# A new layout in device memory for the expert gate values

## What is computed

```python
q = (tok @ wq).reshape(-1, PEER_HEADS, 2, PEER_SUB_DIM)
s1 = jnp.einsum("nhd,kd->nhk", q[:, :, 0], k1)      # 128 keys each side
s2 = jnp.einsum("nhd,kd->nhk", q[:, :, 1], k2)
v1, i1 = lax.top_k(s1, 16);  v2, i2 = lax.top_k(s2, 16)
cand = (v1[..., :, None] + v2[..., None, :]).reshape(-1, 8, 256)
top_s, top_c = lax.top_k(cand, 16)
expert = i1[top_c // 16] * 128 + i2[top_c % 16]
gate = jax.nn.softmax(top_s, axis=-1)
act = jax.nn.gelu(x . u[expert])
out = sum_e (gate * act) * v[expert]
```

## Time and profile before

| | |
|---|---|
| executions timed | 3748.21, 3754.81, 3764.75 us |
| profiled execution, first to last instruction (span) | 3746.2 us |
| TensorE matmul busy | 3568.6 us (95%) |
| TensorE weight load busy | 3086.4 us (82%) |
| VectorE busy | 2356.7 us (63%) |
| ScalarE busy | 1525.1 us (41%) |
| GpSimd busy | 1025.7 us (27%) |
| data moved by DMA | 566.25 MB in 245131 packets |

### The profile page before, as it was taken

How to read it: one execution, slowest core, us unless ns; L and a number is a source line. 1 busy time by engine, 2 the same in 40 slices (tenths; PEclk the granted TensorE clock), 3 DMA queues, 4 the chain that set the end, 5 groups by cost and what they waited for, 6 DMA issues and landing times. The chain is left out here.

```text
span 3746.2 us, 46716 instructions
## 1 busy us (share of the span) xinstructions
PE 3568.6 (95%) x18068; PEld 3086.4 (82%) x18068; DVE 2356.7 (63%) x3934; ACT 1525.1 (41%) x2054; POOL 1025.7 (27%) x678
## 2 busy tenths in 40 slices
PE   7999999979999999999999999999999998699998
PEld 6888777768888889999999999987778887678886
DVE  6655544445469998777657777666565576856354
ACT  5555554445342224444533333335443224434232
POOL 1222222127137775555411111110020014311002
PEclk9999999989999999999999999999999999999999
DMA  5111111036336675677599999861123332132331
GB/s 187 51 51 51 37 51 51 23 133 215 107 103 229 236 242 183 257 261 266 205 332 310 306 312 310 299 214 49 55 91 102 96 96 54 37 98 85 101 96 62
DMA packets 245131, 566.25 MB, mean 151 GB/s; under 512 B 91648, under 2 KB 133904, under 8 KB 242736
## 3 DMA queue, kind: packets, MB, share of 16 engines
q1 hardware_dynamic: 203968, 396.31, 32.9%
q0 software_dynamic: 37440, 135.32, 10.2%
q10 hardware_dynamic: 3504, 31.65, 2.1%
HBM read 497.36 MB, written 60.82 MB: 149 GB/s over the span
## 5 line engine op out<-in xcount | busy, mean ns | idle before, releaser
L1398 PE MATMUL peer_banks<-peer_h_parts,peer_w_parts 128*128 128x448 f32 (+1 forms) x3456 | 735.7, 372 | 11.4 <-POOL peer_w_parts L1679 5.6
L1398 PEld LDWEIGHTS peer_banks<-peer_h_parts,peer_w_parts 128*128 128x128 f32 x3456 | 647.3, 189 | 79.9 <-POOL peer_w_parts L1679 14.2
L1398 PE MATMUL peer_banks<-peer_act_parts,peer_w_parts 128*128 128x448 f32 x3072 | 624.7, 365 | 1.0 <-DVE peer_act_parts L2118 0.8
L1398 PEld LDWEIGHTS peer_banks<-peer_act_parts,peer_w_parts 128*128 128x128 f32 x3072 | 576.4, 188 | 47.1 <-DVE peer_w_parts L2123 1.7
L1851 ACT ACTIVATE peer_w_parts<-slots 128x1024 fp32r<-128x1024 f32 x272 | 287.1, 1056 | 430.0 <-PE peer_banks L1398 415.6
L1398 PE MATMUL ffn_ps<-h_parts,ffn_w_parts 128*128 128x512 f32 x1920 | 441.4, 392 | 18.2 <-DVE h_parts L2736 10.9
L1679 POOL TENSOR_TENSOR peer_w_parts<-slots,peer_w_parts 128x1024 fp32r<-128x1024 f32 x142 | 351.8, 2478 | 337.8 <-ACT peer_w_parts L1851 337.3
L1398 PEld LDWEIGHTS ffn_ps<-h_parts,ffn_w_parts 128*128 128x128 f32 x1920 | 363.1, 189 | 95.1 <-DVE ffn_w_parts L2574 15.5
L1398 PE MATMUL ffn_ps<-ffn_hidden,ffn_w_parts 128*128 128x512 f32 x1920 | 438.1, 390 | 1.5 <-DVE ffn_hidden L2643 1.5
L1398 PEld LDWEIGHTS ffn_ps<-ffn_hidden,ffn_w_parts 128*128 128x128 f32 x1920 | 360.3, 188 | 77.7 <-issue 3.1
L2420 ACT ACTIVATE ffn_w_parts<-slots 128x1024 fp32r<-128x1024 f32 x160 | 168.6, 1056 | 311.9 <-PE ffn_ps L1398 304.5
(11 more groups left out here) (589 smaller groups left out, 5631.3 us busy)
## 6 DMA issues: line engine op xcount, KB each, us to landing
slots<-in_peer_u SPq DMA_DIRECT2D x128, 512.0 KB, 3.6
slots<-in_peer_v SPq DMA_DIRECT2D x128, 512.0 KB, 4.9
slots<-in_mlp_w SPq DMA_DIRECT2D x128, 512.0 KB, 3.5
peer_slab<-in_w_mod POOLq DMA_DIRECT2D x96, 512.0 KB, 5.6
peer_acts<-h SPq DMA_DIRECT2D x128, 224.0 KB, 4.2
peer_gates<-peer_slab ACTq DMA_DIRECT2D x16, 1792.0 KB, 15.4
peer_slab<-peer_acts SPq DMA_DIRECT2D x128, 224.0 KB, 5.1
peer_slab<-peer_gates SPq DMA_DIRECT2D x128, 224.0 KB, 5.5
```

Source lines behind the costliest of these rows:

```text
L1398: last = nc.tensor.matmul(out, w(a, k), x(b, k), start=start and k == ks[0] and n == 0, stop=stop and k == ks[-1] and n == 2)
```

## The change

`gates` in device memory becomes [tile, partition, 448 tokens]. The load of a tile's gate values is then one block: 128 runs of 1792 bytes, one for each partition. The store of a slab quarter is 32 runs of 448 bytes for each partition, 4096 runs in all, where it had 128 runs of 14336 bytes. Bytes, number of DMAs, waits and the order of all instructions are as before.

```diff
-    gates = nc.dram_tensor("peer_gates", (TT, P, NKEY * PT), F32, kind="Internal").ap()
+    gates = nc.dram_tensor("peer_gates", (NKEY, P, DENSE), F32, kind="Internal").ap()
     acts = nc.dram_tensor("peer_acts", (U_TILES, P, DENSE), F32, kind="Internal").ap()
-    g_h = gates.rearrange("b p (i t) -> i p b t", t=PT)
...
                 sp.wait_ge(slab_out[n // 32], 16 * TT)
-                sp.dma_start(gate_in_sb[:, n % 4], g_h[n]).then_inc(gate_in[n % 4], 16)
+                sp.dma_start(gate_in_sb[:, n % 4].rearrange("p b t -> p (b t)"), gates[n]).then_inc(gate_in[n % 4], 16)
...
                         for s in range(4):
-                            act.dma_start(gates[tt][:, s * quarter:(s + 1) * quarter],
-                                          flat[:, s * quarter:(s + 1) * quarter]).then_inc(slab_out[s], 16)
+                            rows_of = slice(s * (NKEY // 4), (s + 1) * (NKEY // 4))
+                            act.dma_start(gates[rows_of, :, tt * PT:(tt + 1) * PT].rearrange("i p t -> p i t"),
+                                          slab[:, rows_of, :]).then_inc(slab_out[s], 16)
```

## The result

The change makes the kernel slower: 3837.38 us (median of four, 3829.18 to 3841.46) against 3751.51 us in the same series, a ratio of 1.0208 with a 95% interval from 1.0186 to 1.0230. The profiled execution of the changed kernel has a span of 3839.7 us, 93.5 more than that of before.

A forecast was written before the change was run, and what follows sets the result against it. TensorE was taken to bound the whole expert layer, with DMA hidden. Loads 0, blocked issues 88 and clock 10 sum to 98 us: 3754.8 + 98 = 3853 us, with an 8-in-10 range of 3778 to 3950.

The forecast's parts named there:

- the sum of 98: Whole kernel's predicted slowdown in us: loads 0, blocked store issues 88, lower clock 10.
- Part 1: Gate loads: longer runs save 41 us of DMA time hidden under TensorE; priced at 0, at best 1 us.
- Part 3: ScalarE's four store issues per token group: each waits until 71 packets an engine remain ahead; TensorE stops 88 us in all.
- second rival: Store issue on ScalarE does not block, only late landing counts: 41 us, 3796 us; chance 0.15.
- The size of the hold: ScalarE held 25.6 us per token group instead of 3.05: 697 runs an engine at 31 ns, about 4 us other traffic.
- The slack: At ScalarE's stores: about 0.7 us more delay is free before TensorE stands still, beside the present 3.05 us of issue.
- Part 4: TensorE after each of four stops: lower clock loses 2.5 us each, 10 in all, between 0 and 20.
- The down stage: Down stage was to keep its length, with its DMA share falling from 0.92 to about 0.86.
- first rival: Each short store write also costs a read: 62 ns a run, 174 us plus 12 for clock, 3941; chance 0.22.
- third rival: Store issue unblocked, 22 ns a run or less, landing in time: not slower, 3754 us; chance 0.09.
- Nothing later waits: Next group's first copy and the pair loads: later waits on the same stores cost nothing more.
- the forecast's own range: Total time from 3822 us (25 ns a run, no clock loss) to 3895 (40 ns, or longer block of 953 runs).

The follow-up runs named there:

- e1: The kernel before with only the gate loads changed to one contiguous 1792-byte run per partition, stores kept long: 3752.75 us, ratio 1.0003.
- e3: The change with one store DMA per token group in place of four, same 16384 runs of 448 bytes: 3805.27 us, ratio 1.0133.
- e6: The change with two store DMAs per token group in place of four: 3815.61 us, ratio 1.0148.
- e4: The kernel before, long runs kept, with ScalarE waiting for its four stores to land right behind their issue: 3841.1 us, ratio 1.0221.
- e2: The change with rows padded so each short store run begins at a multiple of 512 bytes, loads again 448-byte runs: 3820.77 us, ratio 1.0181.
- e5: The change with padded rows, every short run placed to touch three aligned 256-byte blocks: 3845.49 us, ratio 1.0247.
- e7: The change with one store DMA per token group and the 512-byte padding together: 3790.14 us, ratio 1.0092.

## Why the prediction was right

3853 us were predicted, 3837 measured; the sum of 98 stands against 86 between the medians and 93.5 between the spans. The mechanism was the predicted one. That the spans come within 5 us of the sum is in part luck, as the last lines of this section say.

- **Part 1, the loads at 0: right.** e1 measures 1.0003. The DMA share of the down stage went to 0.87, predicted 0.86.
- **Part 3, the blocked issue: right, shown** by the issue times, by e3 and e6 (no list ahead of an issue, no hold; fewer runs ahead, a shorter one) and by e4 (the same hold without short runs, the same loss). The second rival, a queue that takes long lists at once, is out. When the last of the four issues returned, 11324, 11364, 10819 and 11297 packets of the queue had started in the four groups, 708, 710, 676 and 706 for each DMA engine, so that 58 to 92 of the 768 ahead were left; the prediction had 71. The time fits too. In group 0 the hold began 3.7 us before 1512 us; in these the queue of the stores started 79 packets and the other queues 227 (the prediction had 4 us for their traffic). 697 runs at 22.6 ns are 15.8 us more, 19.5 in all, and 19.59 was measured. At 30.5 ns it is 21.3, and 25.0, against 25.34 and 23.93.
- **The size of the hold: too large.** The term of 25.6 us measured 21.8 on average (87.2 / 4). The price of 31 ns a run was that of groups 1 and 2; groups 0 and 3 have 22.6 and 23.8 (10080 packets of the queue in 15 us of group 3). I took the price from loads under a busy queue, and nothing of before told the groups apart.
- **The slack: right.** 3.05 + 0.7 us were taken off; the runs show 3.4 in the change ((87.2 - 73.6) / 4) and 3.5 in e4. TensorE's stop came out at 18.4 us for each group in place of 22, 73.6 in place of 88.
- **Part 4, the clock: right, 7.8 us where 10 were forecast.** That is what the up tiles lost around the four stops, 2.0 us each for the 2.5 taken. In e2, e4, e5 and e6, also with four stops, it is 9.0, 8.6, 10.4 and 9.7 us. So stops of 15 to 22 us cost about as much at the lower clock as the one of 9 us from which the term was read. The reading itself was a little low: a clock of 0.95 over the 9 us behind 2531 is another 0.9 us at the lower level, which makes 2.1 us lost in place of 1.7.
- **The down stage: not as forecast.** It was to have the same length; in the profiled execution its matmuls took 11.8 us more. e4 and e6 show the same (636.5 us), e1, e2 and e5 do not (624.3 to 624.5), whatever their loads, stores and stops. Nor does e3, whose down stage has the change's layout and loads: its 627.0 us have in them the lower clock behind a stop of 10.6 us at their start, and further on it took 202.5 ns a matmul. The cause stays open. Only one execution of each kernel is profiled, so whether the rate changes from one execution to the next, and how much of it is in the 86 us between the medians, is not known.
- **The double price of short writes (first rival): out.** 448-byte runs to device memory cost 22.6 to 30.5 ns, no more than the 31 that the loads gave. The Trainium skill ("DMA: Bandwidth & Descriptors", Specifications) has transfers under 512 bytes done by reading, modifying and writing; these stores show no doubled price, and whether a smaller part of it is that, no run shows, for none stored runs of 512 bytes in this pattern.
- **No change (third rival): out.** It wanted an issue that doesn't block and 22 ns a run or less. e7 has the first and comes near the second (22.8 ns measured in e2), and its time is still 1.0092 of before.
- **Nothing later waits: right, but for 1 us.** No first copy of a group waited for the stores, although those of group 1 took some 43 us to land in place of 36; the first copy came late enough (53 us behind the first issue in group 0). The pair loads came 54.2 us after VectorE was free, and TensorE waited 1.8 us for VectorE's first product parts behind them, where it had waited 0.8.
- **A sum in the prediction:** the lower end of the forecast's own range, 3822 us, is 3826 by its terms (697 · 25 ns, plus 4, minus 3.05 and 0.7, is 17.7 us four times). Nothing rests on it.

The stops were forecast 14 us too long and the clock's term 2 us too large; the down stage's 12 us, which nothing in the prediction has, nearly make up for it in the profiled span. Without them the span would have grown by some 82 us.

## What to carry to other kernels

When a layout change moves short runs from one DMA to another, ask first which engine issues the DMA that gets them, and what stands behind the issue on that engine. Two or more long lists in a row held the engine that issued them here until the ones ahead had nearly drained; one DMA in place of four, with the same bytes and runs, took more than a third of the loss away (1.0208 to 1.0133). Stores issued from SP's queue, which has no computing behind it, were not tried. Shortening a load's list is worth only what its consumer waits, and a DMA share of 0.92 beside a bound engine that never waits was worth nothing.

When the busy time of an engine differs between two profiles, split it by stage before naming a cause. Here 20 us of slower matmuls looked like the clock behind the stops; 12 of them lay in a stage without stops, and a run with the old layout had them too.

## What the runs showed of the hardware that I had not expected

- The price of a short store stepped with the 256-byte blocks that it touches: 22.6 and 22.8 ns a run for two, 30.5 and 30.1 ns for three, with 448 bytes in each case. A start off a multiple of 256 bytes cost nothing where the run touched no third block (group 3: a hold of 18.32 us in the change, 18.18 with aligned runs).
- Recorded packet times overlap: a queue of short runs shows 109 to 119% of 16 engines, so a price is better taken from packets by time than from the share.
- A DMA issue returned in 0.38 us with 1024 runs for each DMA engine in its list, while the same engine's next issue behind only 256 took 7.76 us.
- A stop of TensorE cost, beside itself, 2.0 to 2.6 us at the lower clock (7.8 to 10.4 us over four), whether the four stops came to 45.1 us in all (e6) or to 81.4 (e5).
- At a granted clock of 1.00, TensorE's matmuls of the down stage ran at one of two rates, 202.5 ns each (2468 or 2469 in 500 us: before, e1, e2, e3, e5, e7) or some 206.5 (2411 in 498.22 us in the change, 2417 in 499.45 in e4, 2422 in 500.00 in e6). What chooses between them is open.
